# Token-major rows and a gather by token number for the expert steps of a two-layer backbone

## The reference, cut to what matters

```python
def moe(h, w_router, b_router, w_gate, w_up, w_down):
    t = h.reshape(-1, D_MODEL)
    s = jax.nn.sigmoid((t @ w_router).astype(F32))
    ...  # best group of four experts by its top-2 sum, then the two best experts in it
    combine = jnp.sum(jax.nn.one_hot(eidx, N_EXPERTS, dtype=F32) * wts[..., None], axis=1).astype(t.dtype)
    out = jnp.zeros_like(t)
    for e in range(N_EXPERTS):
        y = (jax.nn.silu(t @ w_gate[e]) * (t @ w_up[e])) @ w_down[e]
        out = out + combine[:, e:e + 1] * y
    return out.reshape(shp)
```

## Time and profile before

| | us |
|---|---|
| median of 3 runs | 1410.79 |
| the runs | 1406.19 to 1416.46 |
| span of the profiled execution, first to last instruction | 1404.0 |
| PE busy | 1247.6 (89%) |
| DVE, ACT, POOL busy | 626.9, 366.2, 124.9 |

### The profile page before, as it was taken

How to read it: one execution, slowest core, us unless ns; L and a number is a source line. 1 busy time by engine, 2 the same in 40 slices (tenths; PEclk the granted TensorE clock), 3 DMA queues, 4 the chain that set the end, 5 groups by cost and what they waited for, 6 DMA issues and landing times.

```text
span 1404.0 us, 20024 instructions
## 1 busy us (share of the span) xinstructions
PE 1247.6 (89%) x8172; PEld 793.1 (56%) x8172; DVE 626.9 (45%) x1126; ACT 366.2 (26%) x595; POOL 124.9 (9%) x119
## 2 busy tenths in 40 slices
PE   3699898899999988999999966987999986999986
PEld 1477576787877733334343325776789852444443
DVE  2628358776547362122131116485885761221222
ACT  2622124433144310000100115433544620000000
POOL 0000000000004020000000011003960201000000
PEclk9799998999999989999999996999999998999998
DMA  9747994242213389899899983775345489999997
GB/s 380 271 186 321 398 387 185 90 91 86 94 61 122 152 326 387 290 354 347 329 356 389 415 338 149 279 321 210 117 111 176 168 343 387 388 383 397 404 415 301
DMA packets 59887, 382.71 MB, mean 273 GB/s; under 512 B 8913, under 2 KB 11413, under 8 KB 20309
## 3 DMA queue, kind: packets, MB, share of 16 engines
q1 hardware_dynamic: 45584, 345.00, 63.2%
q10 hardware_dynamic: 9748, 18.74, 4.1%
q0 software_dynamic: 4464, 17.71, 3.6%
HBM read 363.84 MB, written 44.84 MB: 291 GB/s over the span
## 4 chain that ended last, share of the span: by engine, by line
issue 22%; PE 21%; DMA 11%; DVE 7%; ACT 2%; POOL 2%; SPq 0%; DVEq 0%; POOLq 0%; ACTq 0%
DMA wexp<-in_expert 7%; PE bank L2421 3%; DMA x_rows<-trow,rowid 3%; PE bank L2015 3%; PE bank L2436 3%; PE bank L2017 3%; PE bank L2016 3%; PE bank L1982 2%; PE bank L2454 1%; DVE wlo L1255 1%; POOL x_rows L770 1%; POOL m_lo L754 1%; DMA stage<-in_in 1%; PE bank L2294 1%; PE bank L2107 1%
## 5 line engine op out<-in xcount | busy, mean ns | idle before, releaser
L2421 PE MATMUL bank<-wexp,xg 128*64 128x512 f32 (+1 forms) x1488 | 263.3, 595 | 5.0 <-DMA wexp<-in_expert 1.9
L2015 PE MATMUL bank<-h_hi,whi 128*128 128x512 f32 (+1 forms) x640 | 228.6, 357 | 21.5 <-DVE wlo L1255 13.3
L2016 PE MATMUL bank<-h_lo,whi 128*128 128x512 f32 (+1 forms) x640 | 222.8, 348 | 0.0
L2017 PE MATMUL bank<-h_hi,wlo 128*128 128x512 f32 (+1 forms) x640 | 222.6, 348 | 0.0
L2421 PEld LDWEIGHTS bank<-wexp,xg 128*64 128x64 f32 (+1 forms) x1488 | 77.8, 125 | 155.6 <-issue 145.0
L1255 DVE TENSOR_TENSOR wlo<-stage,whi 128x2048 fp32r<-128x2048 f32 x56 | 134.3, 2405 | 69.8 <-ACT whi L797 68.2
L2436 PE MATMUL bank<-wexp,act_a 128*32 128x256 f32 (+1 forms) x1072 | 145.1, 488 | 16.3 <-DMA wexp<-in_expert 12.2
L2015 PEld LDWEIGHTS bank<-h_hi,whi 128*128 128x128 f32 x640 | 127.2, 199 | 46.2 <-DVE wlo L1255 18.3
L1255 DVE TENSOR_TENSOR act_a<-act_s,bank 128x256 f32<-128x256 f32 (+1 forms) x47 | 17.1, 365 | 263.9 <-ACT act_s L797 263.9
L2016 PEld LDWEIGHTS bank<-h_lo,whi 128*128 128x128 f32 x640 | 127.0, 199 | 13.8 <-issue 0.5
L2017 PEld LDWEIGHTS bank<-h_hi,wlo 128*128 128x128 f32 x640 | 126.4, 197 | 14.0
(11 more groups left out here) (342 smaller groups left out, 1603.4 us busy)
## 6 DMA issues: line engine op xcount, KB each, us to landing
wexp<-in_expert SPq DMA_DIRECT2D x190, 1024.0 KB, 14.6
stage<-in_in SPq DMA_DIRECT2D x40, 1024.0 KB, 8.6
raw<-in_mod SPq DMA_DIRECT2D x18, 1024.0 KB, 7.9
stage<-in_mod SPq DMA_DIRECT2D x16, 1024.0 KB, 4.9
x_rows<-in_c_zero SPq DMA_DIRECT2D x32, 512.0 KB, 11.0
y_rows<-in_c_zero SPq DMA_DIRECT2D x20, 512.0 KB, 12.1
spare<-in_mod SPq DMA_DIRECT2D x8, 1024.0 KB, 14.4
stage<-in_out SPq DMA_DIRECT2D x8, 1024.0 KB, 4.8
```

The lines of the kernel that those rows point to most:

```text
L2015: MM(o, w[0], x_[0], start=start, stop=False)
L2016: MM(o, w[0], x_[1], start=False, stop=False)
L2017: return MM(o, w[1], x_[0], start=False, stop=stop)
L2421: ins = MM(bank[0][g * w:(g + 1) * w, :], x_[:, 2 * j + k, :], weights[:, c], start=(first_ == 0), stop=(last_ == 0))
```

## The change: what it does

- `x_rows` is gone. The shifted rows of `trow` are written once and in token order to `t_rows` (POOL, one 512 KB DMA for each 128 tokens, as soon as DVE has added the shift).
- The scatter keeps its number of indirect DMAs and its indices, but carries the token's number (4 bytes) into `row_tokens[l]` in place of the 4 KB row.
- Once these landed, POOL loads the numbers of the first three steps' rows (`load_tokens`, 4 bytes to each partition), waits, and issues an indirect gather of those rows out of `t_rows` (`gather_rows`), each landing in `xpick`. Then it loads the numbers of all other steps, waits, and gathers one step after the other as ring buffers come free. The overflow loop does the same on POOL.
- ACT issues no row loads any more, and waits at step `PICKED[l] - 1` of the first layer for the writes of `t_rows`.
- SP writes no zeros. POOL zeroes `row_tokens` at the start, and those blocks of `y_rows` that no step writes (9 blocks) while the first layer's gates run, and waits for them there.
- `PICKED` is (2, 2): steps 2 and 3 of the first layer take their rows from the gather. Which ring buffer a step uses is counted from the end (`row_buffer`), and the semaphores of the ring are shared by both layers.

```diff
-PICKED = (4, 2)
+PICKED = (2, 2)
...
+        "token": i[:, None] + 128 * np.arange(8)[None, :],
...
+        token_i = keep("token_i", [P, 4], i32)
+        row_token = keep("row_token", [C, max(len(p.steps) for p in plans) + 1], i32)
...
-        x_rows = [nc.dram_tensor(f"x_rows{l}", (ROWS[l], D), f32, kind="Internal").ap() for l in range(DEPTH)]
-
+        t_rows = nc.dram_tensor("t_rows", (TOK, D), f32, kind="Internal").ap()
+        row_tokens = [nc.dram_tensor(f"row_tokens{l}", (ROWS[l], 1), i32, kind="Internal").ap() for l in range(DEPTH)]
+        UNWRITTEN = range(plans[0].extra_base + E, ROWS[0], P)
...
-        def row_loads(r):
-
-            return (r // XR + (1 if r % XR == XR - 1 else 0)) * 16
+        def row_loads(l, r):
+            b = row_buffer(l, r)
+            before_ = [(i, q) for i in range(l) for q in range(len(plans[i].steps) - PICKED[i]) if row_buffer(i, q) == b]
+            return (len(before_) + 2 * l + r // XR + 1) * 16
+        def result_loads(l, t):
+            rows_ = sum(row_buffer(i, q) == t for i in range(l + 1) for q in range(len(plans[i].steps) - PICKED[i]))
+            return (rows_ + 2 * (l + 1)) * 16
+        def row_buffer(l, r):
+            return (r - (len(plans[l].steps) - PICKED[l]) - 1) % XR
...
-                    if l == 0 and at["in", 4] <= n < at["in", 4] + ROWS[0] // P:
-                        b = n - at["in", 4]
-                        for rows_ in (*x_rows, y_rows):
-                            if b * P < rows_.shape[0]:
-                                load("all", "rows_zeroed", rows_[b * P:(b + 1) * P, :], A["c_zero"])
...
+            pool.wait_ge(sem("all", "const_in"), 2 * 16)
+            p.then(nc.gpsimd.tensor_copy(token_i[:, :], token[:, 0:4]))
+            for tokens in row_tokens:
+                g = tokens.shape[0] // 4
+                load("all", "dram_rows", tokens.rearrange("(a b) o -> a (b o)", a=4), A["c_zero"][0:4, 0:g].bitcast(i32))
+            pool.wait_ge(sem("all", "dram_rows"), DEPTH * 16)
...
+                if l == 0:
+                    for row in UNWRITTEN:
+                        rows_ = y_rows[row:min(row + P, ROWS[0]), :]
+                        load("all", "dram_rows", rows_, A["c_zero"][0:rows_.shape[0], :])
+                    pool.wait_ge(sem("all", "dram_rows"), (DEPTH + len(UNWRITTEN)) * 16)
...
-                    pool.wait_ge(sem("all", "rows_zeroed"), (sum(ROWS) // P + ROWS[0] // P) * 16)
-
-                pool.wait_ge(S("h2"), seqs(l) * KT + T // P)
+                NT = T // P
+                for i in range(NT):
+                    t = row_tile(l, NT + i)[0]
+                    pool.wait_ge(S("h2"), seqs(l) * KT + i + 1)
+                    load("all", "dram_rows", t_rows[t * P:(t + 1) * P, :], trow[:, t, :])
                 pool.wait_ge(S("rowid_ok"), 1)
-                for t in range(T // P):
+                for t in range(NT):
                     for c in range(2):
                         pool.indirect_dma_start(
-                            out=x_rows[l], out_offset=bass.IndirectOffsetOnAxis(ap=rowid[:, 2 * t + c:2 * t + c + 1], axis=0),
-                            in_=trow[:, t, :], in_offset=None,
-                        ).then_inc(sem("all", "scattered"), 16)
-
-                pool.wait_ge(sem("all", "scattered"), sum(2 * (span(i) // P) for i in range(l + 1)) * 16)
-                for i in range(XR - 1):
-                    row, w = plans[l].steps[PICKED[l] + i][3:]
-                    load("all", f"yg{i}", xpick[0:w, i, :], x_rows[l][row:row + w, :])
+                            out=row_tokens[l], out_offset=bass.IndirectOffsetOnAxis(ap=rowid[:, 2 * t + c:2 * t + c + 1], axis=0),
+                            in_=token_i[:, t:t + 1], in_offset=None,
+                        ).then_inc(sem("all", "tokens"), 16)
+                tokens_done = sum(2 * span(i) // P + len(plans[i].steps) - PICKED[i] + 1 for i in range(l)) + 2 * NT
+                pool.wait_ge(sem("all", "tokens"), tokens_done * 16)
+                plan = plans[l]
+                places = [(row, w) for z, use, fill, row, w in plan.steps[PICKED[l]:]] + [(plan.extra_base, E)]
+                LAST = len(places) - 1
+                def load_tokens(r0, r1):
+                    for r in range(r0, r1):
+                        row, w = places[r]
+                        load("all", "tokens", row_token[0:w, r:r + 1], row_tokens[l][row:row + w, :])
+                def gather_rows(r):
+                    w, b = places[r][1], row_buffer(l, r)
+                    landed_ = sem(l, "xloop") if r == LAST else sem("all", f"xload{b}")
+                    pool.indirect_dma_start(
+                        out=xpick[0:w, b, :], out_offset=None, in_=t_rows,
+                        in_offset=bass.IndirectOffsetOnAxis(ap=row_token[0:w, r:r + 1], axis=0),
+                    ).then_inc(landed_, 16)
+                load_tokens(0, XR - 1)
+                pool.wait_ge(sem("all", "tokens"), (tokens_done + XR - 1) * 16)
+                pool.wait_ge(sem("all", "dram_rows"), (DEPTH + len(UNWRITTEN) + sum(span(i) // P for i in range(l + 1))) * 16)
+                for r in range(XR - 1):
+                    gather_rows(r)
+                load_tokens(XR - 1, LAST + 1)
+                pool.wait_ge(sem("all", "tokens"), (tokens_done + LAST + 1) * 16)
+                for r in range(XR - 1, LAST + 1):
+                    pool.wait_ge(S("xT_mm"), PICKED[l] + r - XR + 1)
+                    gather_rows(r)
+                pool.wait_ge(S("items_ok"), 1)
+                count = pool.value_load(count_i[0:1, 0:1], min_val=1, max_val=plan.extra)
+                with pool.Fori(0, count) as i:
+                    pool.wait_ge(S("xT_mm"), i + PICKED[l] + LAST + 1)
+                    pool.sem_inc(sem("all", "passed"), 1)
+                    load(l, "xloop", row_token[0:E, LAST:LAST + 1], row_tokens[l][bass.ds(i * E + plan.extra_base + E, E), :])
+                    pool.wait_ge(S("xloop"), i * 32 + 32)
+                    pool.sem_inc(sem("all", "passed"), 1)
+                    gather_rows(LAST)
...
-                def load_rows(s):
-
-                    row, w = places[s]
-                    r = s - PICKED[l]
-                    act.dma_start(xpick[0:w, r % XR, :], x_rows[l][row:row + w, :]).then_inc(S(f"xload{r % XR}"), 16)
...
-                    if s == PICKED[l] - 1:
-
-                        act.wait_ge(sem("all", "scattered"), sum(2 * (span(i) // P) for i in range(l + 1)) * 16)
...
+                        act.wait_ge(sem("all", "dram_rows"), (DEPTH + len(UNWRITTEN) + sum(span(i) // P for i in range(l + 1))) * 16)
...
-                    if PICKED[l] <= s <= STEPS - XR + 1:
-                        if s > 0:
-                            act.wait_ge(S("xT_mm"), s)
-                        load_rows(s + XR - 1)
...
-                    act.wait_ge(S("xT_mm"), s + 1)
-                    act.dma_start(xpick[0:E, LAST % XR, :], x_rows[l][bass.ds(i * E + plan.extra_base + E, E), :]).then_inc(S(f"xload{LAST % XR}"), 16)
...
-                        if r < XR - 1:
-                            pe.wait_ge(sem("all", f"yg{r}"), l * 48 + 16)
-                        else:
-                            pe.wait_ge(S(f"xload{r % XR}"), row_loads(r))
-                        columns(r % XR, w)
+                        pe.wait_ge(sem("all", f"xload{row_buffer(l, r)}"), row_loads(l, r))
+                        columns(row_buffer(l, r), w)
...
-                    pe.wait_ge(S(f"xload{LAST % XR}"), row_loads(LAST) + i * 16)
+                    pe.wait_ge(S("xloop"), i * 32 + 16)
```

More of the change, by code:

```diff
@@ L86 @@
 for _name, _n in (("ident", 128), ("ones", 128), ("headmean", 128), ("before", 128), ("iota", 64), ("rot", 128),
-                  ("headsum", 2), ("fold", 16), ("first", 36), ("cosT", 256), ("sinT", 256), ("plan", 64), ("halves", 64), ("rowno", 24)):
+                  ("headsum", 2), ("fold", 16), ("first", 36), ("cosT", 256), ("sinT", 256), ("plan", 64), ("halves", 64), ("rowno", 24), ("token", 8)):
     TABLES[_name] = (TABLE_COLS, _n)
@@ L223, in hybrid_backbone @@
         "oh_lo", "pT", "pT_act", "pT_dve", "places", "probs", "pv", "q_g", "q_ok", "q_rot", "q_sq", "q_stat", "ranked", "items_ok", "routed",
-        "diag", "token_of", "parts", "spread", "acc", "row_a", "rows", "rows_ok", "rowid_ok", "xload0", "xload1", "xload2", "xload3", "xT_mm", "xg", "gu_sb", "y_ev", "used00", "used01", "used02", "used03", "used04", "used05", "used10", "used11", "used12", "used13", "used14", "used15", "score", "short", "silu", "tab_in", "u", "uT",
+        "diag", "token_of", "parts", "spread", "acc", "row_a", "rows", "rows_ok", "rowid_ok", "xT_mm", "xg", "gu_sb", "y_ev", "used00", "used01", "used02", "used03", "used04", "used05", "used10", "used11", "used12", "used13", "used14", "used15", "score", "short", "silu", "tab_in", "u", "uT",
         "u_row", "v_ok", "vrows",
@@ L358, in hybrid_backbone @@
         tables = keep("tables", [P, TABLE_COLS])
```

(15 more changed lines are left out.)

## The result

The changed kernel takes **1417.3 us** (median of 20 runs, 1411.1 to 1425.8); the kernel before took 1408.8 in the 20 runs beside it. Ratio 1.0061, 95% interval [1.0046, 1.0076]: 0.6% slower, where I had forecast 6.4 us less. The profiled execution has a span of 1418.7 us against 1404.0; these 14.7 us are more than the 8.5 between the medians. So I use the profiled pair to compare places inside the kernel, and not to compare its ends.

What follows compares the result with a forecast made beforehand. PE, busy 89% of the span, was taken to set the pace, so changes count only where it idles. Terms of -12.5, +8.0 and -1.9 us sum to -6.4 on a median of 1410.8: 1404 us, range 1387 to 1431.

Steps and rivals of the forecast that it cites:

- Part 1: First layer's mixer: the zeros leave SP's queue and PE's waits shrink, -12.5 us, bounds 0 to -16.1.
- (c): First layer's mixer: shorter stalls give back perhaps 1 us of the time lost to a granted clock of 0.70.
- (a): First layer's mixer: the unit loaded at 138.30 us arrives in time without zeros; 4.0 us off.
- (b): First layer's mixer: the load issued at 181.75 loses six zero blocks in front, so the probabilities come earlier; 7.5 us off.
- Part 2: First layer's expert steps: two row selections leave PE, which then waits for the scatter, token load and gather chain; +8.0 us.
- its landing: First layer's last token scatter lands 6.5 us after its issue at 522.4, at 528.9; bounds 2.4 and 28.7.
- 15 us as the sign of a wrong prediction: Token scatter: a landing above 15 us would show the prediction wrong; 5 to 8 us was expected.
- gather: First layer's rows of step 2: 0.3 us for issue and 6.3 to land, arriving at 543.1.
- Part 3: Second layer: scatter, token loads and gather bring the rows at 1181.2 in place of 1183.10, and the end follows; -1.9 us.
- A: Rival, both layers: small transfers land fast, each of the two small hops taking 2.4 us; 1388 us, chance 0.20.
- C: Rival, first layer's mixer: the zeros hid nothing, other chains take the waits over; 1417 us, chance 0.18.
- B: Rival, both layers: each 4-byte row takes its own turn beside weight packets, scatter lands no sooner; 1436 us, chance 0.20.

Runs made afterwards that it cites:

- the table's runs: The changed kernel with scattered numbers of 4 bytes, or rows of 64 or 512, starting 16, 64 or 512 bytes apart: 1394.7 to 1398.6 us.
- the version with four picks: The changed kernel with four picked steps in the first layer again, PICKED (4, 2), tokens scattered and rows gathered as in it: 1401.0 us, ratio 0.9944.

## Why the prediction was wrong, step by step

**Part 1** (forecast -12.5, bounds 0 to -16.1; measured -17.8). The mechanism was right, and `zhy` was named as what is late next. The size was off by 5.3 us, beyond my bound, and the term that was mis-sized is (c), the clock. The waits gave 10.8 us where (a) and (b) had 11.5. The clock gave 6.5 where I had 1, and 3 as its bound: I had read only the stretch from 220 to 230 us, and PE's rows before and after show the slower work behind the other two waits too. The remaining 0.5 us came behind 280 us and is not traced. In (b) I had also counted only the six zero blocks right before the load: the high part came 14.7 us earlier, not 7.5. That bought no more, since PE's waits can only shrink to nothing. The nine blocks on POOL cost nothing, as forecast.

**Part 2**, and here the forecast fell. It was +8.0; measured is 564.87 - (559.57 - 17.81) = **+23.1 us**. By terms:

- issue of the scatters: as forecast, 504.62 is 522.4 less 17.8;
- **its landing: 17.2 for 6.5, +10.7.** This is the step that failed: "Nearest I hold the 128 KB row load beside the weight stream, 6.5 us". As a price of the small transfer beside full engines 6.5 was right: in the table's runs with 16 bytes and more the last scatter took 6.2 to 7.0 us. It failed on the layout: 4-byte numbers side by side. My upper bound of 28.7 took it in, and I had named 15 us as the sign of a wrong prediction;
- token loads and their landing: 8.3 for 7.6, +0.7;
- gather: 9.2 for 6.6, +2.6. The rows of step 2 are 256 KB, and the kernel before loaded that much directly in 7.8 and 9.5 us (the two lines below), a nearer price than the one I took. It varies: in the table's other versions the same gather took 5.1 to 8.4 us;
- from there to step 4: 25.3 for 24.4, +0.9.

```profile
xpick<-x_rows ACTq DMA_DIRECT2D x18, 256.0 KB, 7.8
xpick<-x_rows POOLq DMA_DIRECT2D x3, 256.0 KB, 9.5
```

The sum is +14.9; between 8.0 and 23.1 lie 15.1, and the rest is the time between the landing and POOL's next issue, which I had not counted. PE's stall follows: 32 us for the 19 forecast. With the numbers 512 bytes apart the rest of the sum comes out: PE asks for the rows at 509.41 (525.83 less a wait of 16.42) and reaches the columns of step 4 at 552.11, 42.7 us later, where I had forecast 567.5 - 524.4 = 43.1; in the changed kernel it is 57.3. Step 5 waits for nothing, as forecast. The effect on the range that I had left open for ACT's filter loads is small: with them moved away, PE's rows came at 534.29, 4.2 us sooner counted from the first scatter, and the ratio, 1.0045 [1.0022, 1.0068], cannot be told from the change's own.

**Part 3** (forecast -1.9). PE's rows came at 1193.65. The layer's scatter began 6.1 us later than before; less these it is +4.5. The landing again, 11.85 for 6.5, is 5.3 of the 6.4 us between forecast and measurement.

**The sum with the measured terms** is -17.8 + 23.1 + 4.5 = +9.8; the medians differ by 8.5. So the error of part 1 hid a quarter of those of parts 2 and 3, and that the total lies only 13 us from 1404 is in part luck. With its numbers 16 bytes apart the same kernel took 1398.0 us, ratio 0.992, below my 1404: of the errors in the two directions it has little left but the one in its favour.

**The rivals.** A (1388): the hops don't take 2.4 us beside full engines. In the seven versions with the numbers or rows apart the first layer's last scatter took 3.4 us once and 5.5 to 7.0 otherwise. C (1417) names the very time that was measured and is refuted by the runs with moved zeros: its sum is 0 for part 1 and +6.1 for parts 2 and 3 on a median of 1410.8, where the traces show -17.8 and +27.6 and the median is 1408.8. That it hit the time was luck. B (half way 1420) is nearest to what happened, by another mechanism: I had made its case rest on one packet for each row, and the packets are shared. It did say rightly when it decides: the scatter landed at 521.8 us, which is 539.6 on the time scale of the kernel before (17.8 later), close to its 541. Whether an indirect DMA packs its 4-byte rows as direct ones are packed, which the prediction left open, is settled (33 packets for 128 rows), and it decided nothing. The Trainium skill, *DMA: Bandwidth & Descriptors*, "Why small descriptors are slow (HBM only)", names two fixed costs of a small descriptor, a few cycles for each packet and 32 bytes of descriptor metadata, and none that depends on where its neighbours lie. By these alone 4 bytes apart and 16 bytes apart would cost the same; 17.2 and 7.5 us were measured, and the measurement decides.

**Still open:** why neighbours hold each other up. 4 and 16 bytes were tried, not 8; the size of the table was not varied by itself, and nothing was tried on the order of the indices. Likewise the 8 us that the version with four picks stood above my estimate are only in part accounted for (5 us of new waits in the first layer).

## What to carry to other kernels

Before a scatter is made smaller, look at where its elements land: 4-byte writes side by side in HBM took longer here than rows of 512 bytes (17.2 against 6.9 us) and slowed the weights beside them; give each number a place of its own, 16 bytes or more from the next. Bytes that nobody waits for belong where the engines are idle, not between loads that somebody waits for. And a chain of dependent transfers is paid in full when the steps that covered it are given up: 3.6 us of PE work to pick a step's rows had kept PE busy for the 12 us of that step.

## What the runs showed of the hardware

- Eight indirect DMAs of 128 4-byte numbers each to neighbouring HBM addresses took 26.2 us from first issue to last landing, and the DMA engines moved only 39 to 46 GB/s in some stretches beside them; with the numbers 16 bytes apart they took 16.0 us (of which 9.0 pass until the last is issued), and in the second layer the engines moved 422 GB/s beside four of them. Without the weights beside them four scatters of side-by-side numbers landed in at most 6.2 us.
- Rows of 4 KB, scattered by four such DMAs in the second layer, left the engines at 412 GB/s in all (the kernel before with its zeros moved), and the last landed 15.6 to 16.1 us after its issue; without the weights beside them, in 4.0 us.
- In and behind waits of 5.3 and 5.9 us in the first layer's mixer PE's granted clock was 0.50 (the 1.2 GHz level), and the same eight transposes took 1.97 us in place of 1.07. Three waits of 13.1 us in all went with some 6.5 us more of PE's own work.
- The first three gathers of rows of 4 KB by row number took 7.6 to 9.1 us to land in the changed kernel's first layer, and the later ones 3.1 to 8.3. The direct loads of 256 KB in the kernel before took 7.8 (ACT) and 9.5 us (POOL) in the median, so a gather costs about what a direct load does.
